# Half of two projection tiles moved into the sample attention's end, another order of the routing stage, and sample blocks in four column groups

## What is computed

```python
qkv, z, a, b, nq, kvc, kvs, kvw, ng, mg = _split_proj(x @ w_in)
o_dn, S_new, conv_new = _deltanet_mixer(...)       # 8 heads, delta rule
o_nsa = _nsa_core(...)                             # 16 heads, three branches
h = _merge_branches(o_dn, o_nsa, mg)
xp = _layer_norm(DEEPNORM_ALPHA * xp + hp @ w_out[l], ln1_g[l], ln1_b[l])
xs = _layer_norm(DEEPNORM_ALPHA * xs + hs @ w_out[l], ln1_g[l], ln1_b[l])
# the same with a mixture of experts: 64 experts of hidden width 256, the best 6
# of each token (within the best 4 of 8 groups), and one shared expert
xp = _layer_norm(DEEPNORM_ALPHA * xp + _moe_ffn(xp, *moe_w), ln2_g[l], ln2_b[l])
```

## Time and profile before

| | |
|---|---|
| median of the runs | 1853.29 us |
| profiled execution, its own time | 1853.6 us |
| its span, first to last instruction | 1851.8 us |
| TensorE busy, share of the span | 1733.5 us, 94% |
| VectorE / ScalarE / GpSimd busy | 794.5 / 524.3 / 336.7 us |
| mean granted TensorE clock | 0.971 |
| moved by DMA | 371.70 MB |
| third stage, first matmul | 1142.54 us after the span's start |

### The profile page before, as it was taken

One profiled execution on the slowest core, in us unless ns is written; L12 is line 12 of the kernel. 1 busy time (PEld: TensorE's weight loads), 2 busy tenths in 40 slices (PEclk: granted clock), 3 DMA queues, 4 the chain that ended last, 5 costly groups with the idle time before them and its releaser, 6 DMA issues. The chain is left out here.

```text
span 1851.8 us, 26496 instructions
## 1 busy us (share of the span) xinstructions
PE 1733.5 (94%) x9999; PEld 1149.6 (62%) x9999; DVE 794.5 (43%) x1927; ACT 524.3 (28%) x1245; POOL 336.7 (18%) x352
## 2 busy tenths in 40 slices
PE   8999999999999989899888998999998998999987
PEld 6587777777877868787666764575443443444432
DVE  1054664664664410365887651373222121222216
ACT  2224233233234111465667442020111111111110
POOL 0010210211211210131545550001111111111100
PEclk9999999999999989899899998998999999999998
DMA  8071221221232261152000665938999999999987
GB/s 241 1 221 49 71 73 49 68 75 48 60 82 48 47 185 34 59 182 95 5 1 2 228 227 183 408 129 351 372 420 420 421 419 420 420 419 421 419 341 317
DMA packets 168527, 371.70 MB, mean 201 GB/s; under 512 B 36887, under 2 KB 114703, under 8 KB 143568
## 3 DMA queue, kind: packets, MB, share of 16 engines
q1 hardware_dynamic: 148192, 308.69, 45.2%
q0 software_dynamic: 19728, 60.06, 9.1%
q10 hardware_dynamic: 480, 1.25, 0.2%
HBM read 337.75 MB, written 48.15 MB: 208 GB/s over the span
## 5 line engine op out<-in xcount | busy, mean ns | idle before, releaser
L855 PE MATMUL bank<-xT,arena 128*128 128x272 f32 x1440 | 368.2, 399 | 0.0
L855 PEld LDWEIGHTS bank<-xT,arena 128*128 128x128 f32 x1440 | 259.8, 190 | 62.8 <-issue 16.8
L2838 PE MATMUL bank<-arena,kvt 128*64 128x512 f32 (+1 forms) x816 | 258.2, 617 | 21.4 <-issue 20.6
L2838 PEld LDWEIGHTS bank<-arena,kvt 128*64 128x64 f32 (+1 forms) x816 | 88.3, 150 | 156.1 <-issue 156.1
L2921 PE MATMUL bank<-arena,kvt 128*64 128x512 f32 (+1 forms) x408 | 127.8, 598 | 2.2 <-issue 2.0
L3243 DVE SCALAR_TENSOR_TENSOR kvt<-kvt,arena,bank 128x256 f32<-128x256 f32 x37 | 17.8, 481 | 241.5 <-ACT kvt L3033 241.5
L1276 POOL TENSOR_TENSOR arena<-arena 128x512 f32<-128x512 f32 x40 | 46.3, 1157 | 385.5 <-DVE arena L1367 261.0
L2671 POOL DMA_INDIRECT hT<-x_rows,rows_i x37 | 37.5, 1015 | 359.0 <-DVE rows_i L3174 350.9
L2838 PE MATMUL bank<-xT,kvt 128*64 128x512 f32 (+1 forms) x208 | 93.7, 604 | 9.6 <-issue 9.6
L3033 ACT ACTIVATE kvt<-bank 128x256 f32<-128x256 f32 x37 | 14.2, 383 | 279.2 <-PE bank L2838 279.2
L1641 PE MATMUL bank<-xT,arena 128*128 128x272 f32 x352 | 82.8, 399 | 8.6 <-PEq L163 8.6
(11 more groups left out here) (515 smaller groups left out, 2971.6 us busy)
## 6 DMA issues: line engine op xcount, KB each, us to landing
arena<-in_w_exp_gate SPq DMA_DIRECT2D x51, 1024.0 KB, 21.2
arena<-in_w_exp_up SPq DMA_DIRECT2D x51, 1024.0 KB, 25.1
arena<-in_w_exp_down SPq DMA_DIRECT2D x51, 1024.0 KB, 24.1
arena<-in_w_in SPq DMA_DIRECT2D x48, 512.0 KB, 5.3
kvt<-in_w_exp_down SPq DMA_DIRECT2D x13, 1024.0 KB, 23.6
xT<-in_w_exp_gate SPq DMA_DIRECT2D x13, 1024.0 KB, 21.3
xT<-in_w_exp_up SPq DMA_DIRECT2D x13, 1024.0 KB, 26.0
y_rows<-arena SPq DMA_DIRECT2D x1, 12800.0 KB, 40.1
```

Of the source, the lines that this page charges most:

```text
L855: last = mm(banks[2 * (i % 2) + half][:, 0:HALF], wh[blk % RING][:, k, :], xT[:, k, half * HALF:(half + 1) * HALF], start=(k == 0), stop=( ...
L2838: last = mm(banks[2 + 4 * (t % 2)][cols, :], xgT[:, k, cols], ewgu[i % EBUF][:, :, k], start=(k == 0), stop=(k == KD - 1))
```

## The change

Five things are changed.

1. `kv_sample` writes four groups of 208 columns (32 partitions each, one bank) where there were one of 512 and one of 320; ScalarE saves four pieces.
2. Half of `project` of tiles 0 and 1 (k 4 to 7, both halves) is issued in the second stage as 16 pieces of one k (`first_tiles`), between the steps of the sample attention's end and behind its last matmul. The third stage adds k 0 to 3.
3. The third stage takes the tiles in the order 0, 1, 4, 2, 3. `project_sample` writes four groups of 256 columns into bank 7. Projections are cut in halves of four k, with other work between.
4. The counts are spread: those of the first batch come as soon as its masks are there, and the order of the experts is made and stored ahead of the places, of the gates and of three of the shared expert's blocks.
5. SP loads tile 0 of the input and the two LayerNorm rows before the other tiles.

The diff, cut to its core:

```diff
+ORDER = (0, 1, 4, 2, 3)
+PLACE = [ORDER.index(t) for t in range(NTILE)]
+KVQ = (KVW + 16) // 4
...
                 for k in range(KD):
-                    for half, cols in enumerate(KV_COLS):
-                        last = mm(banks[4 + half][64 * half:64 * half + NS_TOK, 0:cols.stop - cols.start], xT[:, k, NP_TOK:], wkv[:, k, cols],
+                    for part in range(4):
+                        last = mm(banks[4][32 * part:32 * part + NS_TOK, 0:KVQ], xT[:, k, NP_TOK:], wkv[:, k, part * KVQ:part * KVQ + KVQ],
...
+            def first_tiles(lo, hi):
+                for piece in range(lo, hi):
+                    n, k = divmod(piece, 4)
+                    t, half = divmod(n, 2)
+                    if piece == 0:
+                        pe.wait_ge(wout_in[1], 16)
+                    last = mm(banks[n][:, :], hT[:, 4 + k, t * P:t * P + P], wout[1][:, k, half * 512:half * 512 + 512], start=(k == 0), stop=False)
...
                         turn_probs(f)
+                        if f in FIRST_PIECES:
+                            first_tiles(*FIRST_PIECES[f])
                         if f >= 1:
                             chunk_values(f - 1)
+                if x == NCHUNK:
+                    first_tiles(0, 4)
+            first_tiles(9, 10)
             chunk_values(len(PFILLS) - 1)
+            first_tiles(10, 12)
...
+            first_tiles(12, 16)
+            pe.wait_ge(first_banked, 1)
...
-            project(0, 0)
...
+            for t in range(2):
+                project(t, 0, 0, 4)
+                project(t, 1, 0, 4)
+            project_sample()
             turn_rows(0)
+            project(2, 0, 0, 4)
             logits(0)
+            project(2, 0, 4, KD)
             turn_rows(1)
+            turn_rows(4)
+            project(2, 1, 0, 4)
             logits(1)
+            pe.wait_ge(res_ready, 6)
+            logits(4)
+            project(2, 1, 4, KD)
             project(3, 0)
             turn_rows(2)
+            project(3, 1, 0, 4)
             logits(2)
+            project(3, 1, 4, KD)
             shared_in(0, 0, 0)
+            shared_in(0, 0, 1)
+            turn_rows(3)
...
+            norm(0)
+            norm(1)
+            norm(4)
+            best_groups(0, 3, 3)
+            norm(2)
+            best_experts(0, 3)
+            norm(3)
+            best_groups(3, NTILE, 5)
+            best_experts(3, NTILE)
```

More of the change, by code:

```diff
@@ L407, in build @@
         NSTEP_S = FILL_STEP[-1] + 1
+        FIRST_PIECES = {len(PFILLS) - 5 + n: (4 + n, 5 + n) for n in range(5)}
         SLOTS = ((0, 1, 4, 5), (6, 7, 2, 3))
@@ L1065, in save_kv @@
             def save_kv(t):
-                n = P if t < 4 else NS_TOK
-                lo, hi = (banks[4 + (2 * t + half) % 4][64 * half * (t // 4):64 * half * (t // 4) + n] for half in range(2))
+                if t == 4:
+                    sc.wait_ge(kv_banked, 2 * NTILE)
+                    for part in range(4):
+                        rows = banks[4][32 * part:32 * part + NS_TOK]
+                        n = min(KVQ, KVW - part * KVQ)
+                        last = actv(kvt[0:NS_TOK, 4, part * KVQ:part * KVQ + n], rows[:, 0:n], ACT.Copy)
+                    last.then_inc(kv_ready, 1)
+                    actv(ab[0:NS_TOK, 4, :], rows[:, n:KVQ], ACT.Copy).then_inc(kv_ready, 1)
+                    return
+                n = P
+                lo, hi = (banks[4 + (2 * t + half) % 4][0:n] for half in range(2))
                 sc.wait_ge(kv_banked, 2 * t + 1)
@@ L1949, in _ @@
                 for par in range(2):
-                    last = mm(banks[2][halves[par], pair * 64:pair * 64 + 64], orow[:, pair], o_perm[:, par], start=True, stop=True)
+                    last = mm(banks[7][halves[par], pair * 64:pair * 64 + 64], orow[:, pair], o_perm[:, par], start=True, stop=True)
             last.then_inc(of_banked, 1)
+            first_tiles(12, 16)
+            pe.wait_ge(first_banked, 1)
         @block.scalar
@@ L2859, in _, with loads, ahead_of @@
+            pe.wait_ge(res_ready, 10)
+            shared_in(0, 1, 0, 0, 2)
             logits(3)
-            shared_in(0, 0, 1)
-            turn_rows(4)
-            pe.wait_ge(res_ready, 10)
-            shared_in(0, 1, 0)
-            logits(4)
+            def loads(u):
+                mm(banks[5][0:NE, 0:1], mask[:, u], ones[:, 0:1], start=(u == 0), stop=(u == 4))
+                return mm(banks[6][:, 0:NE], ones[:, :], mask[:, u], start=(u == 0), stop=(u == 4))
+            def ahead_of(p):
+                for u in range(p + 1):
+                    last = mm(banks[7][:, p * NE:(p + 1) * NE], (tri if u == p else ones)[:, :], mask[:, u], start=(u == 0), stop=(u == p))
+                return last
@@ L2865, in _ @@
+            mask = rt[5]
+            pe.wait_ge(mask_ready, 2)
+            for u in range(3):
+                loads(u)
+            shared_in(0, 1, 0, 2, KD)
             shared_in(0, 1, 1)
             pe.wait_ge(x1t_ready, 2 * NTILE)
-            shared_in(1, 0, 0)
-            shared_in(1, 0, 1)
-            pe.wait_ge(mask_ready, len(BATCHES) + 1)
-            mask = rt[5]
-            for u in range(NTILE):
-                mm(banks[6][0:NE, 320:321], mask[:, u], ones[:, 0:1], start=(u == 0), stop=(u == 4))
@@ L2885, in _ @@
-            shared_in(1, 1, 0)
+            shared_in(1, 0, 0, 0, 5)
+            pe.wait_ge(mask_ready, 3)
+            loads(3)
+            loads(4).then_inc(cnt_banked, 1)
+            for p in range(3):
+                ahead_of(p)
             pe.wait_ge(perm_ready, 2)
```

185 lines of the change are left out of this document (88 added, 97 removed).

## The result

The changed kernel takes 1838.72 us in the median of 4 runs (1838.56 to 1840.77), the kernel before 1853.22 us in the same comparison (1850.97 to 1853.31). The ratio is 0.9927, 95% interval 0.991 to 0.9944. 19.4 us were forecast, 14.5 were gained. Two more comparisons on other chips gave 0.995 (0.9936 to 0.9963) and 0.992 (0.9905 to 0.9935). The profiled execution is the slowest of the four: 1840.77 us, span 1839.0, against a span of 1851.8 before.

What follows compares the result with a forecast made beforehand. TensorE was taken to lead until about 1302 us, then the DMA engines with a full queue; -4.2 + 6.5 - 18.5 - 3.2 = -19.4 us gave 1834 us, with eight in ten within 1828 to 1843.

Steps and rivals of the forecast that it cites:

- Direction and bound: Up to about 1302 us TensorE leads, then DMA's full queue; the end moves as much as the third turn's `gate_up`.
- Keys and values: First stage, sample's block: four column groups side by side take 2.87 us instead of 7.06, gaining 4.2 us.
- Tail: End of the sample attention: with 16 projection pieces there, the third stage starts 6.5 us later.
- Rival 5: Attention's end: pieces are paid in full, wait and slow clock stay, 5 us more, 1839 us; chance 5%.
- Third stage to the first turn: From the third stage's first product: order stored at 84.4 us, first turn at 103.4 instead of 121.9, gaining 18.5 us.
- The new wait: TensorE at `turn_rows(2)` waits 4.0 us for VectorE's `norm(2)`, plus 1.7 us for the clock.
- First turn at the full clock: First turn's transpositions and `gate_up`: TensorE never idle in front, so no half clock, gaining 3.2 us.
- my case: The forecast's own sum for the whole kernel: 1834 us, 1829 to 1838 with its errors; chance 52%.
- 1 (loads of four groups not hidden, or two at a time): Sample's two four-group blocks: unhidden weight loads cost 4.7 us (1839); two at a time, 6.4 (1840); together 15%.
- 4 (taking turns): Sample's two four-group blocks: groups take turns, blocks last 13.8 and 16.5 us, 1858 us, slower than before; chance 4%.
- 2 (stream's start sets the end): Expert weight stream: the end moves with the stream's start, 23.5 us gained, 1830 us; chance 12%.
- 3 (more half clock): Clock falls at the barrier, 1.6 us, and the wait at `turn_rows(2)` costs 2 more: 1838 us; chance 12%.

Runs made afterwards that it cites:

- e4: Changed kernel with the whole weight stream held until the last shared expert block: 1844.37 us, ratio 0.9963 to the kernel before.
- f4: Changed kernel with the third tile's norm ahead of the first batch's group choice and a shared-block piece ahead of the ranks wait: 1831.48 us, ratio 0.9892.
- e1: Kernel before with only the sample's keys and values put in four groups of 208 columns: 1848.9 us, ratio 0.9977.
- f3: Changed kernel with the first piece of the next shared block ahead of TensorE's wait for the ranks: 1836.97 us, ratio 0.9921.
- g2: Changed kernel with the sample's projection in two groups of 512 columns instead of four of 256: 1840.88 us, ratio 0.9945.
- e3: Changed kernel with the third tile's normalization ahead of the first batch's choice of groups: 1836.33 us, ratio 0.9918.
- g3: Changed kernel with only the second streamed expert's gate and up weights held until the last shared block: 1838.68 us, ratio 0.9921.

## Why the prediction was nearly right, point by point

**Direction and bound: right.** The end did move with the third `gate_up`: between it and the end lie 548.0 to 551.1 us in all executions but two (e4 and f4, 553.3 and 553.2), whether it moved by 20 us or by none. The reason I gave, that the stream's start matters only if the turns want their weights, is incomplete. e4's first three turns were served, and TensorE still waited for weights behind them. Another way to count is by how much the queue has moved when it is full for good: by 1330 us 28.28 MB before, 31.09 in e4, 33.85 after, 38.32 in f4, with ends at 1851.8, 1842.6, 1839.0 and 1830.5 us. A straight line of 1 MB for 2.4 us (420 GB/s) through the first meets all fourteen ends within 2.6 us. As every kernel moves the same 371.70 MB in all, this is bookkeeping more than a cause, and it is hardly a better fit than the third `gate_up` plus 550 us, which meets them within 3.3 us. e4, where the two differ most, ended at 1842.6 us: 2.5 us before the one rule (1845.1) and 3.3 us behind the other (1839.3). That the buffers that `gate_up` frees are what usually limits the sum, while the stream starts early enough to reach them, fits all this and is not tested by itself.

**Keys and values: -4.2 forecast, -4.0 measured** in the block (7.06 less 3.03), -4.1 in e1's median. At stage 2's first product it is 3.4 us in the mean of ten executions (667.1 us against 670.47).

**Tail: +6.5 forecast, +7.1 measured** from the product at L1939 (1121.52) to the stage's start (1147.63), 26.1 us against 19.0. The first piece waited 0.88 us, as forecast (1125.4 less 1124.5); the 0.6 too much stand in the six single pieces, which take 0.95 to 1.06 us each from their start to the next product, where I had put 0.86. Rival 5, pieces paid in full, is out.

**Third stage to the first turn: -18.5 forecast, -15.7 measured.** This is the step that was mis-sized. The new wait came where and as large as forecast (3.75 us against 4.0). Missing were 0.9 us of small items up to `turn_rows(2)` (it came at T + 49.9 instead of 49.0), the wait of 1.11 us for the ranks, for which I had taken VectorE's 2.3 us as hidden, and 1.0 us of half clock behind it in L2808 (6.81 us for the 22 products, 5.78 in f3). With the wait 0.25 us shorter than forecast these make the 2.8. The order was stored at T + 86.4, forecast 84.4, and the first turn came at T + 106.2, forecast 103.4.

**First turn at the full clock: -3.2 forecast, -3.0 measured**, 8.95 us from the first turn to the second against 11.95.

**Stage 3's own start.** -4.2 + 6.5 would put it at 1144.8 us. In the ten profiled executions with this code up to there it lies between 1143.68 and 1149.17, mean 1146.6. At stage 2's first product the ten are 2.1 us apart (666.34 to 668.46); the rest arises in stage 2, which takes 476.6 to 481.4 us. Its granted clock differs from run to run (0.92 to 0.94 from 660 to 1040 us) but doesn't put them in order: the two longest have 0.93. What causes it stays open. The one of the changed kernel was 2.8 us late.

The sum by steps: +5.1 (start), -15.7, -3.0 = -13.6 at the third `gate_up`, against -19.4, and -12.8 at the end: 2.8 us lie in the start's scatter and the tail, 2.8 in the stage up to the first turn, 0.2 in the turn, and 0.8 were lost behind it. The median gained 1.7 us more than this execution, since that was the slowest of four.

**Rivals.** The time alone doesn't tell my case from them: 1838.7 us lies in the whole range (1828 to 1843), but just outside that of my own case (1829 to 1838) and on the numbers of rivals 1 and 3 (1839 and 1838). The traces tell them apart. 1 (loads of four groups not hidden, or two at a time) is out by the block of 64 in 2.96 us and by g2; with it falls, for these shapes, the sentence of the Trainium skill ("TensorE: Matmul & The Clock Gate", Part 3, "The mechanism") that a load overlaps only with products of another row group: all four use the same rows. (The same section of the Trainium skill also lets a load into the background weight buffer go ahead. No run here shows whether that is what happens.) 4 (taking turns) is out by the same rows. 2 (stream's start sets the end) is out as I put it, 20 us of earlier start gave 12.8; but e4's late weights show that it has a share, a few us at most. 3 (more half clock) came true in part: of the two places that I named, the barrier stayed warm and the half clock at `turn_rows(2)` cost 1.8 (0.6 in the transpositions, 1.2 in the products) as in my own sum; the further 1.0 us stood behind the ranks.

## What to carry to other kernels

Where a program goes from a TensorE-led part to a part with a full DMA queue, count megabytes at the border: here an edit ahead of it was worth about what it added to them, at the queue's rate, and two late transfers cost nothing while there were holes behind them. A wait of TensorE often costs its length and a stretch of half clock behind it, and with one of a chain of waits gone the next stretch can be longer (e3: 1.7 us more behind the ranks); test such edits together, as their sum can be larger than their parts (2.9 and 0 us alone, 7 together, where 1.0 of the missing us is f3's own scatter ahead of its edit). Work with no dependence on what is waited for, put into a stage's tail, paid here twice: it filled the waits, and it made the next stage start at the full clock.

## What was not expected of the hardware

With the same code up to there, stage 3 starts up to 5.5 us earlier or later, while from there to the third `gate_up` all three executions of the changed kernel and g3 need 140.7 us, to 0.1 us. Four column groups in fp32, all on the same rows, cost what the columns of one group say, with 64 instructions in 2.96 us. And e4, whose code on TensorE is the changed kernel's, needed 144.6 us: the same dips of the clock behind the same waits were longer (granted 0.50 from 1236.2 to 1240 us, 22 products in 7.94 us against 6.81). f3 has the first of these longer dips as well. No run here explains them.
